# Scores of 64-feature heads over all 128 rows of the array, with zeros in the keys of the other head

## What is computed

```python
# first kind, per layer: 8 heads with selected blocks, 8 with a window, 8 "moba" heads
s_s = jnp.einsum('bghqd,bgqnkd->bghqnk', qc, kg) * scale      # 2 key groups, 4 query heads each
s_w = jnp.einsum('bghqd,bgkd->bghqk', qc, kw) * scale
s_own = jnp.einsum('bhqd,bhkd->bhqk', qc, ko) * scale         # moba, 8 key heads
# second kind, first mixer: 8 differential half heads, 8 stick-breaking heads
sc = jnp.einsum('bhqd,bhkd->bhqk', qb, k).astype(jnp.float32) * scale
z = jnp.einsum('bhqd,bhkd->bhqk', qb, k).astype(jnp.float32) * scale
```

## Time and profile before

| | |
|---|---|
| median of 3 runs | 2040.02 us |
| profiled execution, span | 2037.8 us, first to last instruction |
| profiled execution, its own time | the span and 2.2 us around it, if it took the median |
| PE busy | 1996.7 us (98%) |
| PEld busy | 1774.0 us (87%) |
| DVE busy | 1466.3 us (72%) |
| ACT busy | 1092.8 us (54%) |
| POOL busy | 23.6 us (1%) |
| DMA | 183 GB/s mean |

### The profile page before, as it was taken

The page is one execution under the profiler, slowest core; times in us unless marked ns, Lnnn a source line. Parts: engine busy times, 40 slices in busy tenths (PEclk is TensorE's granted clock), DMA queues, the critical chain, the costliest instruction groups (busy, mean ns, idle before and its releaser), DMA issues. The chain is left out here.

```text
span 2037.8 us, 32169 instructions
## 1 busy us (share of the span) xinstructions
PE 1996.7 (98%) x12934; PEld 1774.0 (87%) x12934; DVE 1466.3 (72%) x2326; ACT 1092.8 (54%) x1732; POOL 23.6 (1%) x46
## 2 busy tenths in 40 slices
PE   7999999999999999999999999999999999999999
PEld 5889988898789988898888779888898899899888
DVE  7887778857787786567757577677667757767774
ACT  3555555535656455545546666555455537855552
POOL 1001000000010000000000000000000000000000
PEclk9999999999999999999999999999999999999999
DMA  9455558765455576555556423455555544235553
GB/s 352 159 200 197 188 186 270 263 211 184 166 203 192 165 234 201 184 188 186 186 175 202 140 101 127 145 186 186 184 186 186 187 167 137 94 125 166 186 176 135
DMA packets 266212, 372.23 MB, mean 183 GB/s; under 512 B 8400, under 2 KB 160336, under 8 KB 266064
## 3 DMA queue, kind: packets, MB, share of 16 engines
q1 hardware_dynamic: 264736, 368.91, 54.1%
q10 hardware_dynamic: 1328, 1.26, 0.2%
HBM read 369.09 MB, written 1.05 MB: 182 GB/s over the span
## 5 line engine op out<-in xcount | busy, mean ns | idle before, releaser
L2302 DVE TENSOR_TENSOR parts<-ring,parts 128x2048 fp32r<-128x2048 f32 (+2 forms) x304 | 676.0, 2224 | 390.7 <-ACT parts L721 390.1
L721 ACT ACTIVATE parts<-ring 128x2048 fp32r<-128x2048 f32 (+2 forms) x304 | 565.5, 1860 | 554.1 <-PE psum L1513 321.6
L1513 PE MATMUL psum<-h,parts 128*128 128x512 f32 x1920 | 676.2, 398 | 0.0
L1511 PE MATMUL psum<-h,parts 128*128 128x256 f32 x1920 | 539.3, 281 | 0.7 <-DVE parts L2302 0.4
L1513 PEld LDWEIGHTS psum<-h,parts 128*128 128x128 f32 x1920 | 361.1, 188 | 87.3
L1511 PEld LDWEIGHTS psum<-h,parts 128*128 128x128 f32 x1920 | 362.4, 189 | 2.4 <-DVE parts L2302 2.2
L1505 PE MATMUL psum<-h,parts 128*128 128x256 f32 (+1 forms) x2088 | 265.0, 285 | 4.5 <-DVE h L2311 2.0
L1505 PEld LDWEIGHTS psum<-h,parts 128*128 128x128 f32 (+1 forms) x2088 | 254.0, 190 | 7.2 <-issue 4.9
L1505 PE MATMUL psum<-parts,h 128*128 128x512 f32 (+1 forms) x864 | 203.3, 386 | 5.7 <-DVE h L2311 3.3
L1505 PE MATMUL psum<-hid_hl,parts 128*128 128x256 f32 x1584 | 189.3, 282 | 0.8 <-DVE parts L2302 0.6
L1505 PEld LDWEIGHTS psum<-hid_hl,parts 128*128 128x128 f32 x1584 | 187.9, 189 | 2.4 <-DVE parts L2302 2.4
(11 more groups left out here) (265 smaller groups left out, 2119.3 us busy)
## 6 DMA issues: line engine op xcount, KB each, us to landing
ring<-in_w_ffn_in SPq DMA_DIRECT2D x88, 512.0 KB, 4.8
ring<-in_ffn_w_gate SPq DMA_DIRECT2D x88, 512.0 KB, 3.7
ring<-in_ffn_w_up SPq DMA_DIRECT2D x88, 512.0 KB, 4.7
ring<-in_w_ada SPq DMA_DIRECT2D x43, 1024.0 KB, 5.4
ring<-in_w_in SPq DMA_DIRECT2D x36, 1024.0 KB, 5.0
ring<-in_ffn_w_down SPq DMA_DIRECT2D x32, 1024.0 KB, 5.0
ring<-in_w_ffn_out SPq DMA_DIRECT2D x16, 1024.0 KB, 5.2
ring<-in_ffn_w_down SPq DMA_DIRECT2D x16, 768.0 KB, 4.4
```

The costliest lines, as they stand in the source:

```text
L721: act.activation(out, in_, func, **kw).then_inc(*sig(name, *keys))
L1511: pe.matmul(bank[:, 0:S], wt_hl[1], act[:, 0, :], start=start, stop=False, skip_group_check=True)
L1513: return pe.matmul(bank.rearrange("p (a s) -> p a s", a=2), wt_hl[0], act, start=False, stop=stop, skip_group_check=True)
L2302: dve.tensor_tensor(out, a, b, op).then_inc(*sig(name, *keys))
```

## The change

The products of a 64-feature head now take all 128 partitions. The moving or fixed operand that holds the keys gets one copy per head parity: the rows of the own head hold the keys, the other 64 rows hold zeros. The queries are taken as they are, both heads; the zeros cancel the other one. Columns, order and number of PE's instructions stay as they are.

For this ACT copies each key tile in two halves of 64 partitions into two places (`half_copies`), in place of one copy of 128. POOL writes the zeros. The window keys get an own area (`kw_area`), the selected keys take its old place, the odd moba keys lie where the compressed branch had its values (`feat` 5856 to 6880), and in the differential mixer the two padded tiles `ab_t[:, 1]` and `ab_t[:, 3]` serve the differential keys first and the stick-breaking keys later.

```diff
+        kw_area = sb("kw_area", [P, 2 * S])
...
-        ks_t, kw_t, kc_t = feat[:, 1024:1280], feat[:, 1280:1536], feat[:, 1536:1568]
+        kc_t = feat[:, 1536:1568]
+        ks_pad, kw_pad = (a.rearrange("p (g s) -> p g s", g=2)
+                          for a in (feat[:, 1024:1536], kw_area[:]))
...
-        mk_t = feat[:, 2624:3648].rearrange("p (j s) -> p j s", s=S)
+        mk_pad = [feat[:, a:a + 1024].rearrange("p (j s) -> p j s", s=S) for a in (2624, 5856)]
...
+        ab_pad = [ab_t[:, a] for a in (1, 3)]
...
-                        n=n, q=nq_t[HD * g:HD * g + HD, j, :], k=k_t[HD * g:HD * g + HD, :],
+                        n=n, q=nq_t[:, j, :], k=k_pad[:, g, :],
...
-                    n=n, q=ab_t[HD * (n % 2):HD * (n % 2) + HD, 0, n // 2, :],
-                    k=ab_t[HD * (n % 2):HD * (n % 2) + HD, 1, n // 2, :],
+                    n=n, q=ab_t[:, 0, n // 2, :], k=ab_pad[n % 2][:, n // 2, :],
...
+            pool.memset(kw_pad[HD:P, 0, :], 0.0).then_inc(*sig("pool_zeros"))
+            pool.wait_ge(*own("pool"))
+            pool.memset(kw_pad[0:HD, 1, :], 0.0).then_inc(*sig("pool_zeros"))
...
+                if l:
+                    pool.wait_ge(*at(("x", ("ffnout", l - 1), DC - 1)))
+                else:
+                    for panel in ADA_OUTSIDE:
+                        pool.wait_ge(*at(("released", panel)))
+                pool.wait_ge(*own("pool"))
+                pool.memset(ks_pad[HD:P, 0, :], 0.0).then_inc(*sig("pool_zeros"))
+                pool.wait_ge(*own("pool"))
+                pool.memset(ks_pad[0:HD, 1, :], 0.0).then_inc(*sig("pool_zeros"))
+                pool.wait_ge(*own("pool"))
+                pool.memset(mk_pad[0][HD:P], 0.0).then_inc(*sig("pool_zeros", ("key zeros", l)))
+                pool.wait_ge(*own("pool"))
+                pool.wait_ge(*at(("full", ("cmp out", l, 1))))
+                pool.memset(mk_pad[1][0:HD], 0.0).then_inc(
+                    *sig("pool_zeros", ("odd key zeros", l)))
...
+            pool.wait_ge(*at(("x", ("ffnout", 2), DC - 1)))
+            pool.memset(ab_pad[0][HD:P], 0.0).then_inc(*sig("pool_zeros"))
+            pool.wait_ge(*own("pool"))
+            pool.memset(ab_pad[1][0:HD], 0.0).then_inc(*sig("pool_zeros", "stick zeros"))
...
+            def half_copies(job, even, odd):
+
+                act.wait_ge(*at(("full", job)))
+                for half, dst in enumerate((even, odd)):
+                    r = slice(HD * half, HD * half + HD)
+                    n = dst.shape[1] * (dst.shape[2] if len(dst.shape) == 3 else 1)
+                    src = psum[r, tally.bank(job), 0:n]
+                    if len(dst.shape) == 3:
+                        src = src.rearrange("p (a b) -> p a b", b=S)
+                    run(dst[r], src, ACT.Copy, "act_copied",
+                        *([("copied", job), ("free", job)] if half else []))
...
-                copies(("tr ks", l), ks_t)
+                act.wait_ge(*at(("key zeros", l)))
+                half_copies(("tr ks", l), ks_pad[:, 0, :], ks_pad[:, 1, :])
...
-                        copies(("tr kw", l), kw_t)
+                        half_copies(("tr kw", l), kw_pad[:, 0, :], kw_pad[:, 1, :])
...
+                        act.wait_ge(*at(("odd key zeros", l)))
                         for j in range(2):
-                            copies(("tr mk", l, j), mk_t[:, 2 * j:2 * j + 2, :])
+                            half_copies(("tr mk", l, j), *(a[:, 2 * j:2 * j + 2, :]
+                                                           for a in mk_pad))
...
+                act.wait_ge(*at("stick zeros"))
                 for j in range(2):
-                    copies(("tr ab", 1, j), ab_t[:, 1, 2 * j:2 * j + 2, :])
+                    half_copies(("tr ab", 1, j), *(a[:, 2 * j:2 * j + 2, :] for a in ab_pad))
...
-                        pe.matmul(b[:, 0:S], zk[r, i // 2, 0:P], zq[r, i // 2, :], start=True,
+                        zk = ab_pad[i % 2]
+                        pe.matmul(b[:, 0:S], zk[:, i // 2, 0:P], zq[:, i // 2, :], start=True,
                                   stop=True)
```

More of the change, by code:

```diff
@@ L510, in nsa_heads @@
         def nsa_heads(kind):
-            k_t, c_v = (ks_t, C_VS) if kind == "slc" else (kw_t, C_VW)
+            k_pad, c_v = (ks_pad, C_VS) if kind == "slc" else (kw_pad, C_VW)
             first = 4 if kind == "slc" else 6
@@ L521, in nsa_heads, with paired @@
             return out
-        def paired(q_t, k_t, v):
-            return [dict(n=n, q=q_t[HD * (n % 2):HD * (n % 2) + HD, n // 2, :],
-                         k=k_t[HD * (n % 2):HD * (n % 2) + HD, n // 2, :],
+        def paired(q_t, k_pad, v):
+            return [dict(n=n, q=q_t[:, n // 2, :], k=k_pad[n % 2][:, n // 2, :],
                          v=[v[:, t, HD * n:HD * n + HD] for t in range(TT)],
@@ L558, in attention_of @@
             if kind == "moba":
-                return paired(mq_t, mk_t, tok_in[:, :, C_VB:C_BR]), con("causal"), HD ** -0.5
+                return paired(mq_t, mk_pad, tok_in[:, :, C_VB:C_BR]), con("causal"), HD ** -0.5
             if kind == "diff":
@@ L1170, in diff_mixer @@
                 more = beside()
-                def late_copies(a, scale=None):
-                    for j in range(2):
-                        copies(("tr ab", a, j), ab_t[:, a, 2 * j:2 * j + 2, :], scale)
                 for i in range(len(heads) + LAG + 1):
@@ L1185, in diff_mixer @@
                     if i == 8:
-                        late_copies(2, HD ** -0.5)
+                        for j in range(2):
+                            copies(("tr ab", 2, j), ab_t[:, 2, 2 * j:2 * j + 2, :], HD ** -0.5)
                     if i == 9:
-                        late_copies(3)
+                        for j in range(2):
+                            half_copies(("tr ab", 3, j),
+                                        *(a[:, 2 * j:2 * j + 2, :] for a in ab_pad))
                     if i < len(heads):
@@ L2077, in diff_mixer @@
                 more = kv_steps(0)
-                zq, zk = ab_t[:, 2], ab_t[:, 3]
+                zq = ab_t[:, 2]
                 for i in range(11):
@@ L2081, in diff_mixer @@
                         b = open_bank(("z", i), ATT if i < 2 else stick)
-                        r = slice(HD * (i % 2), HD * (i % 2) + HD)
-                        pe.matmul(b[:, 0:S], zk[r, i // 2, 0:P], zq[r, i // 2, :], start=True,
+                        zk = ab_pad[i % 2]
+                        pe.matmul(b[:, 0:S], zk[:, i // 2, 0:P], zq[:, i // 2, :], start=True,
                                   stop=True)
-                        pe.matmul(b[:, S:S + P], zk[r, i // 2, P:S], zq[r, i // 2, P:S],
+                        pe.matmul(b[:, S:S + P], zk[:, i // 2, P:S], zq[:, i // 2, P:S],
                                   start=True, stop=True).then_inc(
```

## The result

The changed kernel takes 2042.99 us (median of 20 runs, 2036.70 to 2047.19), the kernel before 2040.05 (20 runs, 2037.81 to 2041.64). The ratio is 1.0014, its 95% interval 1.0009 to 1.002. I had forecast 2028.7 and a range of 2021 to 2037. The change costs some 3 us instead of winning 11.

A forecast was written before the change was run, and what follows sets the result against it. PE, busy 98% of the span, was taken to bound the kernel, with 21.8 us to be had. Mixers 10.2 + differential 1.4 + stick-breaking 0.5 - POOL 0.8 = 11.3 us, from 2040.0 to 2028.7; range 2021 to 2037.

The forecast's parts named there:

- are shorter than the 2.34 that led to it, so I add no dip.: New PE waits of 1 to 1.3 us near 99, 118 and 1127 cause no clock dip: nothing charged.
- The four half copies of the moba keys in place of two cost ACT about 1 us; ACT has 42 idle us here, and I cost them at nothing.: First mixer, heads 7 to 23: the extra ACT copies hide in idle time, 0 us.
- The window-key copies: First mixer, before the compressed scores: a second half copy on ACT ends PE's wait 0.26 us later.
- the POOL term: POOL's zero memsets slow DVE beside them: 0.8 us lost, from a span of 0 to 3.5.
- The price of a head: PE saves 0.34 us per 64-row head: 0.20 inside, 0.09 ahead, 0.05 behind.
- The wait near 118: First mixer: savings of heads 4 and 5 fall into a new PE wait of some 0.5 us.
- A longer wait keeps this dip: Stick-breaking heads: the half-clock dip of 3.4 us after PE's 2.34 us wait for DVE stays, some 1.7 us lost.
- where I had 5.1: Each layer's first mixer: 0.3 us from heads 0 to 6 plus 4.8 from heads 7 to 23.
- A (nearly all arrives, 2020): Whole kernel: DVE and ACT less serial than they look, 20 us won, 2020 us; chance 0.16.
- B (DVE binds): DVE binds through the whole mixer, heads 7 to 23 give nothing, 1.7 us won, 2038.3 us; chance 0.15.
- C (slow zeros): POOL's memsets before the differential keys take 34 ns a column, ACT and PE stand 35 us, 2064 us; chance 0.04.
- D (bare loads): Weight loads of 128-row scores run with nothing beside them and eat the head's saving, 2045.5 us; chance 0.02.

The follow-up runs named there:

- experiment 6: Changed kernel with moba copies earlier, window-key copies later, first moba and differential heads waiting for fewer key tiles: 2029.03 us; with idle filler products on PE 2026.98 us.
- experiment 2: Changed kernel with idle filler products on PE before the compressed scores, first moba head and first differential head: 2034.65 us, ratio 0.9973.
- experiment 5: Kernel before with scores over all 128 rows, no zeros or half copies, so heads are not separated: 2029.63 us, ratio 0.995.
- experiment 4: Changed kernel with all zeros and half copies, but scores over 64 rows again: 2052.18 us; with idle filler products in its waits 2045.05 us.
- experiments 1: Changed kernel with ACT's moba half copies moved from behind head 15's exponentials to the top of that step: 2031.09 us, ratio 0.9964.

## Why the prediction was wrong

**The step that failed: "are shorter than the 2.34 that led to it, so I add no dip."** It has two faults. The wait near 99 was not 1.2 us but 2.10. The prediction's own terms give 1.9 (0.60 + 3 x 0.34 + 0.26); its 1.2 holds the saving of one head, where it speaks of heads 0, 1 and 2. And 2.34 was no bound: I had read one wait with a dip behind it and taken its length for the least that does it, while the rows I stood on held no wait between 1.01 and 2.34 without one. The runs show dips behind 1.17 (ahead of the mixers), 1.42, 1.46, 1.50, 1.59, 1.63 (the one left in experiment 6, ahead of a token product), 1.92, 2.10 and 2.19 us, in some executions and not in others. More rows would not have helped: the trace of the kernel before holds a wait of 1.42 us that is not among my rows, with no dip behind it, and it would have seemed to bear the bound out:

```profile
474.65 4.33 PE L1505 MATMUL psum<-parts,h 128*128 128x512 f32 x18 [1.42 <-DVE h L2311]
```

In the profiled execution the new dips took 6.8 us, over the medians some 8 (experiment 2).

**The second: "The four half copies of the moba keys in place of two cost ACT about 1 us; ACT has 42 idle us here, and I cost them at nothing."** The idle time was real, but it lay ahead of the copies, where ACT waited for PE and then for DVE (2.87 and 1.73 us), and not behind them, where PE waited for ACT. The waits there are 2.20 + 1.92 = 4.1 us. Not all of it is the price of the half copies: with whole copies (experiment 5) a wait of 0.76 us is left in layer 0. I had named the cover and not asked on which side of the copies it lay. Also, four half copies took 2.43 us, 0.61 each, where I had put a half at the price of a whole one (0.49 from start to start).

**The window-key copies**, costed at 0.26 us more, took 0.54 more (0.80 for 0.26), and in experiment 4 the wait behind them grew by 0.86 (0.60 to 1.46). Where the other 0.32 come from is open.

Together for the profiled execution: the span came out at 2038.6 where I had 2026.5, 12.1 us more. New dips are 6.8 of it and moba waits 4.1. For the rest I set the starts of PE's products before and after side by side. The first mixers fell short by another 2.4: the early heads by 0.6 in each layer, since the compressed keys came 0.9 us later, counted from the start of the mixer, and not 0.26; the remainder lies behind them. The differential and stick-breaking heads fell short by 0.4. Against that stand the POOL term (0.8) that wasn't lost, and 0.9 us won ahead of the mixers, at a wait for DVE (before, and below it after):

```profile
42.49 5.69 PE L1505 MATMUL psum<-parts,h 128*128 128x512 f32 x24 [1.37 <-DVE h L2311]
41.55 5.70 PE L1549 MATMUL psum<-parts,h 128*128 128x512 f32 x24 [0.38 <-DVE h L2355]
```

The change doesn't touch that place, and in the twelve profiles the wait lies anywhere from none to 1.58 us: these 0.9 us are luck. The 2.10 us of the compressed wait are no loss on top of these: 0.60 were there before, 0.60 are what heads 0 to 2 had saved, and 0.90 are the later keys.

**What held.** The price of a head: 0.65 us for 128-row scores, 0.20 less inside. The wait near 118 (0.5 expected, 0.47). The longer stick-breaking wait (2.52 for 2.34), in the profiled execution with its one dip; but "A longer wait keeps this dip" is no rule, since the wait of 2.51 or 2.52 us stands without a dip in the profiles of experiments 1 and 2, of experiment 6 before its fillers, and of the kernel with the moba wait filled alone.

**What held in part.** At the DVE wait behind the layer's feed-forward start (324.30 after, 326.64 before) layer 0 is 2.3 us ahead, but 0.9 of it are those won ahead of the mixer. So the mixer won 1.4, and without the moba wait of 2.20 it would have won 3.6, where I had 5.1. The differential heads start 1.54 us after PE's last filler there, 1.4 more than before, where I had put 0.98; a half copy took 0.61 us there too. The whole sum of 11.3 us stands beside 11.1 with held clocks. That the two agree so closely is luck: experiment 6 has moved copies and other waits than the ones I took off, and with the copies in place it was 3.5. Nor do runs of the kernel before agree to 0.01%, as three of them did: twenty lie between 2037.81 and 2041.64.

**The rivals.** A (nearly all arrives, 2020) did not come in any version, 2027.0 was the best. B (DVE binds) is refuted by experiment 5, where the gain came through with the same DVE list. C (slow zeros) is refuted by 0.93 ns a column. D (bare loads) is refuted by the loads' rows. By the Trainium skill (SBUF — State Buffer, section "Who interferes with whom") the POOL term was to be 0, and the trace agrees in the one split that zeros ran beside: 2.28 us for DVE's split with and without a memset beside it. No rival held the real mechanism, a clock that falls behind new waits.

**Still open.** In which execution a wait is followed by a dip, and whether for 3.4, 6.8 or 10.2 us, I can't say: the same wait in the two layers of one execution did both. Length alone doesn't decide it. The wait of 474.65, 1.41 to 1.43 us in all twelve profiles, has no dip behind it in any, while the 1.42 us at the compressed scores in experiment 5 had one of 6.82 in both layers. That the clock is lost by these waits is shown by the fillers; what else it takes is not.

## What to carry to other kernels

When a shorter engine list makes other engines late, cost the new waits twice: by their length and by the clock that may fall behind them. Rows of one execution that show a clock dip behind a long wait give no safe length for shorter ones; a few idle products in the wait, over several runs, tell how much of the time is clock. And idle time hides an added instruction only if it lies between that instruction and the one who waits for it.

## What was not expected of the hardware

- The stretches at 0.50 lasted 3.41, 6.82 or 10.24 us. The twelve profiles hold 17 of them ahead of PE's last product, and each begins in or within 1.8 us behind a PE wait of 1.17 to 2.52 us. But without the first wait of each, the profiles hold some 80 waits of 1.17 us or more, so most were followed by none.
- A copy of 64 partitions out of PSUM is no cheaper than one of 128, and here, two from one bank in a row, each was dearer from start to start: 0.40 us for 256 columns (0.26 for the whole copy), 0.61 for 512 (0.49).
- A memset of 64 x 1024 takes 0.95 us, 0.93 ns a column, against 3.4 for POOL's table products, and DVE beside it kept its pace.
